# Two routers: where the scaled token rows are written, and how the expert gathers read them

## The reference

```python
x = x + hier_moe(rmsnorm(x, ln_ffn[layer]), ...)

g_logits = xt @ w_rg + b_rg                      # 4 groups
p_g = softmax(g_logits)[argmax]                  # top-1 group
e_logits = (xt @ w_re + b_re)[chosen group]      # 8 experts of it
top_p, top_j = top_k(softmax(e_logits), 2)
gate = p_g * top_p / sum(top_p)
out = sum over the two experts of gate * ((silu(h @ w_gate[e]) * (h @ w_up[e])) @ w_down[e])
```

## Time and profile before

| | |
|---|---|
| median of 3 runs | 1279.02 us |
| the profiled execution | 1277.85 us, of it the span 1275.9 us |
| instructions | 28285 |
| PE busy | 988.6 us (77%) |
| PEld busy | 759.4 us (60%) |
| DVE busy | 335.3 us (26%) |
| ACT busy | 272.4 us (21%) |
| POOL busy | 36.3 us (3%) |
| HBM read | 455.58 MB |
| DMA over the span | mean 359 GB/s |
| gathers, L988: loads / matmuls | 123.5 / 124.2 us busy, 512 each |
| gate and up matmuls, L1004 | 289.7 us busy |
| down matmuls, L1029 | 157.2 us busy |

### The profile page before, as it was taken

How to read it: one execution, slowest core, us unless ns; L and a number is a source line. 1 busy time by engine, 2 the same in 40 slices (tenths; PEclk the granted TensorE clock), 3 DMA queues, 4 the chain that set the end, 5 groups by cost and what they waited for, 6 DMA issues and landing times.

```text
span 1275.9 us, 28285 instructions
## 1 busy us (share of the span) xinstructions
PE 988.6 (77%) x12800; PEld 759.4 (60%) x12800; DVE 335.3 (26%) x711; ACT 272.4 (21%) x544; POOL 36.3 (3%) x68
## 2 busy tenths in 40 slices
PE   5989978867585858675999999978777575767774
PEld 3877656656463636453888887767556453646542
DVE  3556411111111111012754564311111111111111
ACT  3654400100000100002545354411000000100001
POOL 2033100000000000000000000000000000000000
PEclk9999999999887979897899999999889797979788
DMA  9536879999999999999954453989999999999994
GB/s 306 220 126 259 337 329 424 425 425 427 427 426 426 426 425 426 428 426 368 402 196 165 168 194 132 379 359 426 429 424 426 427 425 427 427 426 426 427 425 205
DMA packets 55321, 458.46 MB, mean 359 GB/s; under 512 B 4976, under 2 KB 14384, under 8 KB 30496
## 3 DMA queue, kind: packets, MB, share of 16 engines
q1 hardware_dynamic: 54512, 455.06, 86.4%
q0 software_dynamic: 688, 1.58, 0.6%
HBM read 455.58 MB, written 1.05 MB: 358 GB/s over the span
## 4 chain that ended last, share of the span: by engine, by line
PE 51%; DMA 42%; DVE 3%; issue 3%; ACT 1%; POOL 0%; SPq 0%; DVEq 0%; ACTq 0%; PEldq 0%; POOLq 0%
DMA ring<-in_w_down 37%; PE wk L988 10%; PE wk L1004 7%; PE wk L1029 6%; PE wk L658 4%; PE wk L662 4%; PE wk L661 4%; DMA ring<-in_w_in_o 4%; PE total L972 3%; PE wk L645 2%; PE total L658 2%; PE total L661 2%; PE total L662 2%; DMA ring<-in_w_in_e 1%; PE total L834 1%
## 5 line engine op out<-in xcount | busy, mean ns | idle before, releaser
L1004 PE MATMUL wk<-ring,xg 128*32 128x128 f32 x8192 | 289.7, 301 | 130.5 <-DMA ring<-in_w_up 59.3
L1004 PEld LDWEIGHTS wk<-ring,xg 128*32 128x32 f32 x8192 | 250.5, 121 | 177.1 <-DMA ring<-in_w_up 69.2
L1029 PE MATMUL wk<-ring,hidT 128*32 128x256 f32 x2048 | 157.2, 457 | 109.5 <-DMA ring<-in_w_down 72.5
L1029 PEld LDWEIGHTS wk<-ring,hidT 128*32 128x32 f32 x2048 | 73.4, 127 | 179.4 <-issue 158.2
L988 PEld LDWEIGHTS wk<-sel,xn 128*128 128x128 f32 x512 | 123.5, 334 | 10.6 <-issue 9.9
L1768 DVE TENSOR_TENSOR hid<-wk,act_g 128x128 f32<-128x128 f32 x64 | 24.0, 375 | 389.2 <-ACT act_g L1371 389.2
L988 PE MATMUL wk<-sel,xn 128*128 128x128 f32 x512 | 124.2, 401 | 2.4 <-PE wk L1029 2.4
L1371 ACT ACTIVATE act_g<-wk 128x128 f32<-128x128 f32 x64 | 17.8, 278 | 442.2 <-PE wk L1004 442.2
L1779 DVE COPY ye<-wk 32x256 f32<-32x256 f32 x128 | 54.3, 424 | 203.2 <-PE wk L1029 202.3
L1378 ACT ACTIVATE ye<-wk 32x256 f32<-32x256 f32 x128 | 47.8, 374 | 279.5 <-PE wk L1029 278.7
L1517 DVE TENSOR_TENSOR slot_parts<-ring,slot_parts 128x1024 fp32r<-128x1024 f32 (+1 forms) x80 | 97.9, 1274 | 26.5 <-ACT slot_parts L1194 26.1
(11 more groups left out here) (275 smaller groups left out, 980.6 us busy)
## 6 DMA issues: line engine op xcount, KB each, us to landing
ring<-in_w_gate SPq DMA_DIRECT2D x64, 2048.0 KB, 45.2
ring<-in_w_down SPq DMA_DIRECT2D x64, 2048.0 KB, 46.1
ring<-in_w_up SPq DMA_DIRECT2D x64, 2048.0 KB, 47.3
ring<-in_w_in_o SPq DMA_DIRECT2D x8, 2048.0 KB, 9.7
ring<-in_w_in_o SPq DMA_DIRECT2D x8, 1024.0 KB, 11.4
ring<-in_w_out_o SPq DMA_DIRECT2D x4, 2048.0 KB, 8.9
ring<-in_w_in_e SPq DMA_DIRECT2D x3, 2048.0 KB, 20.5
ring<-in_w_out_e SPq DMA_DIRECT2D x2, 2048.0 KB, 10.8
```

What stands on the lines that cost most here:

```text
L1004: last = nc.tensor.matmul(wk[0][32 * j:32 * j + 32, part * P:(part + 1) * P], xe[:, k, :], w_[:, k, j * P:(j + 1) * P], start=(k == 0), st ...
L1029: last = nc.tensor.matmul(wk[3][32 * j:32 * j + 32, 0:256], hidT[:, k, :], wd[:, k, j * 256:(j + 1) * 256], start=(k == 0), stop=(k == 3))
```

## The change

ACT no longer scales `xn` in place. It writes the scaled rows to a new tile `rows`, which lies where `xnT` was, and puts them in order of feature blocks: [token, chunk, block, 128 features]. It reads `xn` with a stride of 8 floats for that and writes contiguously. Since this overwrites `xnT`, ACT waits until PE has finished the router logits (`lg`) in place of waiting for each chunk's transposes. The gathers read their stationary operand from `rows`, where a block is 128 neighbouring floats. `xg`, `sel` and `gsel` move to the 2048 floats of `xn`, which nobody reads after the scaling; so DVE waits for the second scaling (`xs1`) before `choose(0)` writes there. What is computed stays the same.

```diff
--- before.py
+++ after.py
@@ -207,9 +207,10 @@
         yl = at(10 * UNIT + 3072, "y_low", [P, TC, 4, P], F32R)
 
 
-        xg = at(AT_A, "xg", [P, DC, 4 * SLOTS])
-        sel = at(AT_A + 1024, "sel", [P, TC, PER, SLOTS])
-        gsel = at(AT_A + 1536, "gsel", [P, TC, PER, SLOTS])
+        rows = at(AT_A, "scaled_rows", [P, TC, DC, P])
+        xg = at(AT_XN, "xg", [P, DC, 4 * SLOTS])
+        sel = at(AT_XN + 1024, "sel", [P, TC, PER, SLOTS])
+        gsel = at(AT_XN + 1536, "gsel", [P, TC, PER, SLOTS])
         act_g = at(AT_A + 2048, "act_g", [P, P])
         hid = at(AT_A + 2176, "hid", [P, P])
         hidT = at(AT_A + 2304, "hidT", [P, 4, SLOTS])
@@ -986,7 +987,7 @@
                                     for k in range(4):
                                         for c in range(TC):
                                             last = nc.tensor.matmul(
-                                                b[:, k * P:(k + 1) * P], every_eighth(xn[:, c, :], 4 * half + k),
+                                                b[:, k * P:(k + 1) * P], rows[:, c, 4 * half + k, :],
                                                 sel[:, c, 4 * quad:4 * quad + 4, :].rearrange("p e s -> p (e s)"),
                                                 start=(c == 0), stop=(c == TC - 1))
                                     last.then_inc(m["gath_ready"], 1)
@@ -1342,10 +1343,10 @@
                 root(e_, 1, ms)
                 preload(ACT.Exp)
                 act.wait_ge(dve_s, V.at(f"{e_}:rs"))
+                act.wait_ge(pe_s, PE.at(f"lg{l}"))
                 for c in range(TC):
-                    act.wait_ge(pe_s, PE.at(f"{e_}:xT{2 * c + 1}"))
-                    nc.scalar.activation(xn[:, c, :], xn[:, c, :], ACT.Copy, scale=rstd[:, c:c + 1]
-                                         ).then_inc(act_s, A.done(f"{e_}:xs{c}"))
+                    nc.scalar.activation(rows[:, c, :, :], xn[:, c, :].rearrange("p (a k) -> p k a", k=DC), ACT.Copy,
+                                         scale=rstd[:, c:c + 1]).then_inc(act_s, A.done(f"{e_}:xs{c}"))
                 act.wait_ge(dve_s, V.at(f"gd{l}"))
                 for c in range(TC):
                     last = nc.scalar.activation(t4[:, c, :], t4[:, c, :], ACT.Exp, accum_out=sg4[:, c:c + 1])
@@ -1738,6 +1739,7 @@
                         ins = tt(sel[:, c], pl, slots, ALU.is_equal)
                     ins.then_inc(m["sel_ready"], 1)
 
+                dve.wait_ge(act_s, A.at(f"{e_}:xs1"))
                 choose(0)
                 dve.wait_ge(rounds_set[l], 1)
                 for n in ("hid_done", "g_copied", "y_copied"):
```

## The result

The changed kernel takes 1270.69 us (median of 4 runs, 1267.87 to 1271.35) against 1278.57 us before (4 runs, 1277.07 to 1279.52): a ratio of 0.9937, 95% interval 0.9924 to 0.9949. The forecast was 1270.3 us, with a range of 1267.5 to 1276. The profiled execution is the fastest of the four, 1267.87 us with a span of 1266.1.

What follows compares the result with a forecast made beforehand. The prediction took saturated DMA as the bound, broken once per layer by a stop behind the first gather. Its terms, -4.1 - 4.1 + 0.1 = -8.1 us, led to a forecast of 1270.3 us, range 1267.5 to 1276.

Steps and rivals of the forecast that it cites:

- What bounds: Expert loops: DMA is saturated except for one stop per layer; only each layer's first gather is exposed, the other fourteen not.
- The gathers: Gather loads on PE: contiguous reads 0.11 us apart, a gather of 3.6 us instead of 7.7, giving 4.1 us.
- rival B: Gather loads: the stride is not what makes them slow, gather stays at 7.7 us, 1278 to 1279 us; chance 0.08.
- Layer 0: Stop of transfers in layer 0, some 7 us: the first gather's gain fits in whole, -4.1 us.
- Layer 1: Stop of transfers in layer 1: the gap of 4.7 us shrinks to 0.6, -4.1 us.
- ScalarE's scaling: Scaling in the router, now a strided read: the pair takes 2.17 to 3.9 us, costing 0.1 us for both layers.
- prediction's own slack: Layer 0, sel ready before PE's filling ends: of 0.5 us delay, 0.1 to 0.2 us reach the gather.
- bound from PE's load: Upper end for ScalarE's scaling, from the strided load's 1.9 ns per element: 3.9 us for the pair.
- Rival A: PE instruction-supply stalls ahead of the first release: 3.1 us for one, 6.2 for one per layer; 1273 to 1276 us; chance 0.13.
- Rival C: Router: strided scaling on ScalarE delays the exponentials and becomes the bound; about 1282 us at five times the duration; chance 0.04.
- PE's busy time: PE in the whole kernel: busy time some 60 us smaller, with the same 425 GB/s in both saturated stretches.
- The sum: Whole kernel: -4.1 for layer 0, -4.1 for layer 1, +0.1 for the scaling, together -8.1 us.

Runs made afterwards that it cites:

- e3: Changed kernel with the other fourteen gathers issued twice, the first of each layer once: 1270.91 us, ratio 0.9941 to the kernel before.
- e2: Changed kernel with the first gather of each layer issued twice: 1278.12 us, ratio 0.9998 to the kernel before.
- e1: Changed kernel with the stride put back: ScalarE writes rows in token order, gathers read every eighth element; 1277.41 us, ratio 0.9989 to the kernel before.
- e9: Changed kernel plus test instructions behind the output with strides of 1, 2, 4 and 8 floats on PE, ScalarE and VectorE; single run, not read for time.
- e5: Changed kernel with the first gather issued twice in layer 0 alone: 1274.25 us, ratio 0.9969 to the kernel before.
- e4: Changed kernel with ScalarE's scaling reading xn contiguously and writing rows with a stride of 128 floats: 1270.19 us, ratio 0.9939 to the kernel before.
- e6: Changed kernel with the first gather issued twice in layer 1 alone: 1274.83 us, ratio 0.9965 to the kernel before.
- e7: Changed kernel with ScalarE writing each chunk of rows twice: 1279.08 us, ratio 1.0017 to the kernel before.
- e8: Changed kernel without the two filling matmuls, keep_running(2), ahead of the expert loop: 1273.35 us, ratio 0.9965 to the kernel before.
- e11: Changed kernel with five filling matmuls in place of three behind the router logits, and one in place of two later: 1269.61 us, ratio 0.9938.

## Why the prediction was right, step by step

- **What bounds.** Right: gathers beside saturated transfers are free (e3, 0.2 us for 50), the first of each layer is paid in full (e2, 7.4 us for 7.2).
- **The gathers.** 0.11 us apart and 3.6 us forecast, 0.116 and 3.73 measured; the gain is 4.0 us in layer 0 and 3.8 in layer 1 (7.64 to 3.83), not 4.1. Taking the contiguous 128-column load of L1014 as the measure was what made it exact. The stride as the cause, argued then from one pair of rows, is shown by e1 and e9; rival B is out.
- **Layer 0.** -4.1 forecast; unit 11 is 3.96 us earlier behind the transposes, the stop is 3.7 us shorter (7.7 to 4.0), and e5 prices that way at 3.6 us for 3.6 us, with the reservation made there.
- **Layer 1.** -4.1 forecast, with 0.6 us of stop left. In the usual course unit 11 comes 3.9 us earlier (19.4 for 23.3) and some 1.1 to 1.4 us of the 5.0 us of stop stay (e3, e4), more than the 0.6 forecast; with the clock at its high level, as in the profile of after, the stop is gone.
- **ScalarE's scaling.** The duration was outside the bounds: 2146 ns where 1132 to 1.9 ns x 1024 = 1950 were given, 4.18 us for the pair against at most 3.9. Its term in the sum, 0.1 us, came close by luck: ScalarE starts 0.4 us before VectorE, not with it, and its exponentials follow one another in 0.6 us (151.46 to 152.03), not 0.8, so that VectorE is 0.1 us late where 0.5 was worked out, and the gather not at all. (By the prediction's own slack, 156.17 - 155.70 = 0.47 us, its 0.5 us would have left 0.0 and not 0.1 to 0.2.) The bound from PE's load was of the right kind, since both slow down between the same strides (e9), but ScalarE pays more for an element, 2146 / 1024 = 2.1 ns and not 1.9.
- **Rival A.** PE's stalls without a cause stand behind the first release in the profile of after (2.29 us at 177.7, 3.29 us at 188.1), where units already under way cover them, as the stalls of before were (3.11 and 2.76 us). Ahead of the first release there is none: unit 11 of layer 0 leaves 18.1 us behind the transposes in after, e3, e4 and e6 alike. What makes the stalls was not tested.
- **Rival C.** A real mechanism, not reached. With T = 8.4 us its formula gives 7.2 us and e7 measured 8.4, 1.2 times as much (1.4 times the 6.1 us of the changed kernel's rows).
- **PE's busy time.** Some 60 us less were forecast, 47 came (988.6 to 941.6). The gathers gave their 62, but the gate and up matmuls went from 289.7 to 303.8 us, at a granted clock of 0.86 and 0.84 in the saturated stretches where it was 0.89 and 0.87. That this comes from PE having less to do is borne out by e3: with fourteen gathers doubled they take 291.6 us, while the other runs with fast, single gathers there have 301 to 309. It lies beside the transfers and cost nothing, but a forecast of PE's busy time has to count it.
- **The sum.** -8.1 us forecast, -7.9 measured between the medians. So close a match is partly luck: e1 gives the stride 6.7 us and leaves 1.1 us, whose cause is open, while the forecast had put all of it down to the gathers.

## What to carry to other kernels

Ask of a faster engine only where its work stands in front of the release of something that has run dry: here 2 of 16 equal gathers carried the gain, and the other 14, with 54 of the 62 us saved in the gathers, bought nothing that could be measured. A transposition or an interleaved layout can be paid by whichever engine has room beside the chain: the strided pass cost ScalarE 2 us once a layer in place of 4 us of PE for every gather. Work taken off PE in front of a release can let its clock fall; the next 3.7 us of matmuls then took 5.2 to 5.8 (e7, e8).

## What the hardware showed that I had not expected

- A float32 stride of 2 on SBUF is nearly free (196 for 192 ns of load), one of 4 is at the full price (330 ns), 8 adds next to nothing (334 ns). PE's moving side has the same step: 275 to 405 ns a matmul.
- Writing with a stride costs ScalarE what reading does (1.15 and 1.16 us for 512 elements at a stride of 4, 0.61 without), and VectorE goes from 0.41 to 0.64 us.
- PE came to the gather at the 1.2 GHz level after 1.4 us without work (granted clock 0.50, e8), but a rest does not decide by itself: in e11 the gather behind 0.44 us took 5.46 us and the one behind 0.75 us took 3.83. The second filling of the changed router ran at either level in different executions (1.96 us in the profile of after, 3.51 in that of e3).
